# Attention of the sampled rows: forget terms, new keys and new values of four sequences in one product each, key transposes between the score products

## What is computed

```python
def _sample_attention(q, k, v, logf, cache_k, cache_v, cache_logf, page_table):
    ...
    k_all = jnp.concatenate([kp, k], axis=1)
    v_all = jnp.concatenate([vp, v], axis=1)
    f_cum = jnp.cumsum(jnp.concatenate([lp, logf], axis=1), axis=1)
    ...
    out = _attend(q, k_all, v_all, f_cum[:, past:], f_cum, q_pos, k_pos)

def _attend(q, k, v, fq, fk, q_pos, k_pos):
    s = jnp.einsum('nqhd,nkhd->nhqk', q, k).astype(jnp.float32) * (HEAD_DIM ** -0.5)
    s = s + jnp.swapaxes(fq, 1, 2)[..., :, None] - jnp.swapaxes(fk, 1, 2)[..., None, :]
    mask = k_pos[None, :] <= q_pos[:, None]
    s = jnp.where(mask, s, -jnp.inf)
    p = jax.nn.softmax(s, axis=-1)
    return jnp.einsum('nhqk,nkhd->nqhd', p.astype(v.dtype), v)
```

## Time and profile before

| what | value |
|---|---|
| median of three runs | 4012.2 us (4010.51 to 4014.12) |
| profiled execution: its own time | 4016.07 us |
| its span | 4014.3 us |
| mean granted TensorE clock | 0.892 |
| PE busy | 3120.4 us (78%) |
| DVE busy | 2461.1 us (61%) |
| ACT busy | 1553.2 us (39%) |
| POOL busy | 1241.3 us (31%) |
| HBM | 1271.34 MB read, 321 GB/s over the span |

### The profile page before, as it was taken

One profiled execution on the slowest core, in us unless ns is written; L12 is line 12 of the kernel. 1 busy time (PEld: TensorE's weight loads), 2 busy tenths in 40 slices (PEclk: granted clock), 3 DMA queues, 4 the chain that ended last, 5 costly groups with the idle time before them and its releaser, 6 DMA issues. The chain is left out here.

```text
span 4014.3 us, 44298 instructions
## 1 busy us (share of the span) xinstructions
PE 3120.4 (78%) x11756; PEld 1457.5 (36%) x11756; DVE 2461.1 (61%) x6411; ACT 1553.2 (39%) x4273; POOL 1241.3 (31%) x1139
## 2 busy tenths in 40 slices
PE   8799979567886887688678868886887688757777
PEld 2466653243243234224332433242335234411331
DVE  0222221458768758766876677677757775856685
ACT  0233320125534543444255335534552454333333
POOL 0000011013333343443344334433443334334333
PEclk9688889678988999899889989997998899889879
DMA  8211122359998999999999999999999899989998
GB/s 319 77 37 37 37 87 111 120 199 353 408 346 329 409 409 386 370 412 387 386 375 411 390 372 368 405 404 355 400 411 365 351 404 406 376 332 418 371 375 363
DMA packets 299715, 1291.67 MB, mean 322 GB/s; under 512 B 39271, under 2 KB 135415, under 8 KB 163125
## 3 DMA queue, kind: packets, MB, share of 16 engines
q0 software_dynamic: 156672, 1124.27, 69.6%
q1 hardware_dynamic: 142780, 164.51, 12.5%
HBM read 1271.34 MB, written 17.79 MB: 321 GB/s over the span
## 5 line engine op out<-in xcount | busy, mean ns | idle before, releaser
L1647 PE MATMUL YY<-ring,dg 128*64 128x512 f32 (+1 forms) x4224 | 1742.0, 663 | 574.4 <-ACT dg L1218 552.2
L1089 POOL DMA_INDIRECT ring<-experts_dram,idxc x1056 | 1192.0, 1129 | 1925.7 <-PE YY L1647 1721.0
L1492 DVE CUSTOM_DVE_ANT_0 ring<-ring,h2c 128x1024 f32<-128x1024 f32 x1056 | 1266.0, 1225 | 543.0 <-DMA ring<-experts_dram,idxc 533.9
L1647 PEld LDWEIGHTS YY<-ring,dg 128*64 128x64 f32 (+1 forms) x4224 | 519.0, 148 | 1643.9 <-ACT dg L1218 922.6
L1208 ACT ACTIVATE ga<-act 128x1 f32<-128x1 f32 x1056 | 212.1, 201 | 1007.8 <-DVE act L1492 1006.0
L1218 ACT ACTIVATE dg<-fold,gw 128x64 f32<-128x64 f32 x1024 | 356.0, 348 | 50.0 <-PE YY L1647 1.1
L1628 PE MATMUL M<-fT,wq 128*128 128x128 f32 (+1 forms) x2304 | 303.5, 295 | 87.2 <-DMA wq<-w_query_dram 87.2
L1628 PEld LDWEIGHTS M<-fT,wq 128*128 128x128 f32 x2304 | 295.2, 211 | 92.1 <-DMA wq<-w_query_dram 90.8
L1210 ACT ACTIVATE gw<-ga,gc 128x1 f32<-128x1 f32 x1056 | 311.1, 295 | 35.3 <-ACT ga L1208 1.2
L1243 DVE SCALAR_TENSOR_TENSOR yac<-win,cw,yac 128x128 f32<-128x128 f32 x960 | 262.8, 347 | 0.0
L530 PE MATMUL A<-w_in,hT 128*128 128x512 f32 (+1 forms) x432 | 213.8, 660 | 0.0
(11 more groups left out here) (305 smaller groups left out, 2612.6 us busy)
## 6 DMA issues: line engine op xcount, KB each, us to landing
wq<-w_query_dram SPq DMA_DIRECT2D x72, 1024.0 KB, 19.7
wa<-w_ada_dram SPq DMA_DIRECT2D x12, 2048.0 KB, 8.0
ring<-experts_dram,idxc POOLq DMA_INDIRECT x1056, 13.1
w_in<-w_in_dram SPq DMA_DIRECT2D x1, 10272.0 KB, 33.2
kh<-kT_scratch SPq DMA_DIRECT2D x16, 264.0 KB
xb<-x_prompt_dram SPq DMA_DIRECT2D x8, 512.0 KB, 5.3
t_xb<-x_prompt_dram SPq DMA_DIRECT2D x8, 512.0 KB, 11.1
w_o<-w_o_dram SPq DMA_DIRECT2D x8, 512.0 KB, 4.9
```

Source lines behind the costliest of these rows:

```text
L1089: pool.indirect_dma_start(ring[:, k % RING, :], None, I["experts"], bass.IndirectOffsetOnAxis(idxc[:, k:k + 1], 0)).then_inc(g_in[k % RING ...
L1492: v.tensor_tensor_reduce(out=u, in0=u, in1=h2, scale=1.0, scalar=0.0, op0=ALU.mult, op1=ALU.add, accum_out=act8[:, k % RING:k % RING + 1]) ...
L1647: mm = pe.matmul(YY[o, half * 512:(half + 1) * 512], dg[:, k % DG, 0:w], ring[:, k % RING, D + half * 512:D + (half + 1) * 512], start=(k ...
```

## The change

Per group of four sequences instead of per sequence: the forget products (now L811 and L813), the products with the new keys (L816, L817) and those with the new values (L832), each with 128 stationary columns. `Lb` is laid out so that the four sequences of a group lie side by side for each page. `score(n)` becomes `turn(n, c)`, four transposes of one chunk, `meet(n, c)`, one score product, and `forget(g)`. PE's loop transposes chunk c of sequence n and then multiplies chunk c of sequence n − 1. `s_done` is raised after the last score product of a sequence and after `forget(g)`, ten times in all, and the numbers waited for follow that. The products with the values of one sequence now follow those of the sequence before directly.

```diff
-        Lb = sb("Lb", [P, NS * NP, H, QS])
+        Lb = sb("Lb", [P, 2, NP, 4, H, QS])
...
                     if n >= 2:
-                        act.wait_ge(s_done, n - 1)
+                        act.wait_ge(s_done, n - 1 + (n - 2) // 4)
...
-                    own.step(v.tensor_copy(Lb[:, NP * n + j, :, :],
+                    own.step(v.tensor_copy(Lb[:, n // 4, j, n % 4, :, :],
...
                     if n >= 2:
-                        v.wait_ge(s_done, n - 1)
+                        v.wait_ge(s_done, n - 1 + (n - 2) // 4)
...
             def soft(g):
-                v.wait_ge(s_done, 4 * g + 4)
+                v.wait_ge(s_done, 5 * g + 5)
...
-            def score(n):
+            def turn(n, c):
+
+                if c >= 2 or n >= 1:
+                    last = 2 * n + c // 2
+                    pe.wait_ge(kt_dve if c % 2 == 0 else kt_act, last)
+                for j in range(NP):
+                    mm = pe.transpose(T[c % 2][:, j * P:(j + 1) * P], pages[:, NP * n + j, c * P:(c + 1) * P], ident[:, :])
+                mm.then_inc(kt_done, 1)
+
+            def meet(n, c):
                 g, o = n // 4, slice(32 * (n % 4), 32 * (n % 4) + 32)
-                hq = lambda a, m: a[:, m, :, :].rearrange("p h q -> p (h q)")
-                pe.wait_ge(page_in[n], 16 * NP)
+                pe.wait_ge(kt_dve if c % 2 == 0 else kt_act, 2 * n + c // 2 + 1)
+                mm = pe.matmul(SG[g][o, :], Qbd[:, c, n, :, :].rearrange("p h q -> p (h q)"), KT[:, n % 2, c, :],
+                               start=(c == 0), stop=False, skip_group_check=True)
+                if c == CC - 1:
+                    mm.then_inc(s_done, 1)
+
+            def forget(g):
+
+                four = lambda a: a[:, 4 * g:4 * g + 4, :, :].rearrange("p n h q -> p (n h q)")
+                for j in range(NP):
+                    pe.matmul(SG[g][:, :], Lb[:, g, j, :, :, :].rearrange("p n h q -> p (n h q)"),
+                              later[:, 384 - P * j:896 - P * j], start=False, stop=False, skip_group_check=True)
+                pe.matmul(SG[g][:, :], four(L), ones5[:, :], start=False, stop=True, skip_group_check=True)
+                so = OWN[g][:, 0:TS]
                 for c in range(CC):
...
+                    pe.matmul(so, four(Qbd[:, c]), kT[:, c, :], start=(c == 0), stop=False)
+                pe.matmul(so, four(L), later32[:, :], start=False, stop=True).then_inc(s_done, 1)
...
                     for j in range(NP):
-                        pe.matmul(OG[o, :], PT[:, g, j, o], pages[:, NP * n + j, DA:2 * DA], start=(j == 0), stop=False)
-                    mm = pe.matmul(OG[o, :], PTo[:, g, o], vs[:, :], start=False, stop=True)
-                mm.then_inc(o_done, 1)
+                        pe.matmul(OG[o, :], PT[:, g, j, o], pages[:, NP * n + j, DA:2 * DA], start=(j == 0), stop=False,
+                                  skip_group_check=True)
+                pe.matmul(OG[:, :], PTo[:, g, :], vs[:, :], start=False, stop=True, skip_group_check=True).then_inc(o_done, 1)
...
-            for n in range(NS):
-                score(n)
+            for n in range(NS + 1):
+                if n < NS:
+                    pe.wait_ge(page_in[n], 16 * NP)
+                for c in range(CC):
+                    if n < NS:
+                        turn(n, c)
+                    if n:
+                        meet(n - 1, c)
+                if n % 4 == 0 and n:
+                    forget(n // 4 - 1)
                 if n == 5:
                     values(0)
             values(1)
```

More of the change, by code:

```diff
@@ L788, in _ @@
             pe.matmul(OG[:, :], hrow[:, :], hcol[:, :], start=True, stop=True).then_inc(masks_done, 1)
-            def score(n):
-                g, o = n // 4, slice(32 * (n % 4), 32 * (n % 4) + 32)
-                hq = lambda a, m: a[:, m, :, :].rearrange("p h q -> p (h q)")
-                pe.wait_ge(page_in[n], 16 * NP)
-                for c in range(CC):
[L796 to L812, removed]
```

## The result

The changed kernel takes 3961.6 us (median of four runs, 3957.3 to 3964.3) against 4011.4 (four runs, 4010.0 to 4014.1): a ratio of 0.9873, 95% interval 0.9852 to 0.9893. It gained 49.7 us where 43.6 were forecast. The direction and the place were right; the size was 6 us short, and the median lies at the very edge of the range that began at 3961. By the ratio of the runs, 0.9873 of the 4012.2 that was given, it is 3961.2. That this is just inside is luck: the edge stood for free changes of shape, short passes at their old pace and the runs' spread, and neither of the first two came.

What follows compares the result with a forecast made beforehand. TensorE was taken to set the pace of the `sampled` stage. Terms 29.1 + 12.1 − 2.0 + 9.4 − 5.0 = 43.6 us gained, giving a median of 3968.6 us; range 3961 to 3976, carried to 3982 for two rivals.

Steps and rivals of the forecast that it cites:

- Where it lies and what bounds it: The closed stage `sampled`, 148 of 4014 us: TensorE sets its pace, and what it gains the whole program gains.
- Forget term and new keys: Once per four sequences: eight blocks of 5.04 us go, two of 5.6 come; gain 29.1 us.
- Transposes between products: Score products interleaved with the next sequence's transposes: gain 12.1 us, less 2.0 for new holes and 5.0 for shape changes.
- So the holes of sequences 1 to 7 go: PE's waits for KT copies vanish through interleaving: six of 1.67 us and 2.13 for sequence 6, gain 12.1.
- New values: In values(g), products with new values once per four sequences: 4.7 us per group, gain 9.4, crossings between column quarters included.
- Three crossings: 1.3: In values(g), each crossing between column quarters lays one pass over another, 0.44 us each, read from the last stage.
- nothing: Other end for the crossings in values(g): no overlap of column quarters, 2.6 us less gain.
- The new hole of sequence 5: Before its third lot of transposes, PE waits because soft(0) stands ahead of keys(5) on DVE: 1.4 us lost.
- the wait at the start: Sequence 1's transposes must wait for its pages, 599.7 where sequence 0's products started at 599.13: 0.6 us lost.
- Dear changes of shape: Rival, 6%: each of the 56 changes between transposes and score products costs 0.31 us, 12.4 more, 3981.0 us.
- No hiding: Rival, 6%: key copies come too late for interleaving to hide transposes; 12.1 us not gained, 2.0 not spent, 3978.7 us.
- The clock: Rival, 4%: transposes between products keep TensorE at 1.2 GHz; 64.6 us lost if throughout, 4033.2 us.

Runs made afterwards that it cites:

- bare_turns: Changed kernel with all sixteen transposes of a sequence before its four score products again, the rest as changed; stage 94.56 us against 96.70.
- one_quarter: Changed kernel with all page products of values(g) written to the first 32 partitions of OG, one column quarter; stage 108.66 us against 96.70.
- pairs: Changed kernel reworked: sequences two at a time through two banks, values(g) with page loop outside, softmaxes moved; stage 74.13 us against 96.70, median 3946.2 us.
- values_old: Changed kernel with the products with the new values per sequence again, as before the change; stage 112.40 us against 96.70.

## Why the prediction was right or wrong

**Where it lies and what bounds it: right.** TensorE paced the stage, and 49.15 of the 49.7 us are in it. By undoing the parts, the new values gave 6.3 us more than forecast, the forget term and the turns 0.4 and 0.9 less.

**Forget term and new keys: right.** 29.1 forecast, 28.7 by undoing it. The block is 6.03 us, not 5.6: the rows give 3.63 for the four products with `later`, 1.05 for that with `ones5`, 1.01 for eight short passes (0.126 each, where I had 0.11) and 0.34 for the last two with the change back.

**Transposes between products: a sum that came near by luck, with the wrong reason.** 12.1 − 2.0 − 5.0 = 5.1 forecast, and undoing both halves gives 6.3 − 2.1 = 4.2. The step that failed is "So the holes of sequences 1 to 7 go", where it puts all of them down to the interleaving. They did go, but of the 1.67 us of a sequence, 0.85 were the wait for all four copies ahead of a product that needs the first; the moved wait takes them away in either order, 6.3 us in the stage. The interleaving itself hides the other hole, and pays for it with 28 pairs of changes at 0.275 us, 7.7 us instead of 5.0, with the hole behind `soft(0)`, and with the start: the first score product comes 5.64 us after the first transposes (590.06 to 595.70), since the pages of sequence 1 must land before it, where in bare_turns it comes after 3.82 (588.04 to 591.86). It loses 2.1 us. Nor did I see that a rival lay there: this half of the change was worth doing without. For the change from transposes to products I had 0.06 us from the four transposes followed by one of 32 columns; that was from one transpose to another. From a transpose to a product it is 0.585 − 0.43 = 0.155. Why these two differ, no run tells apart.

**New values: the term that was mis-sized.** 9.4 forecast, 15.7 measured by undoing it (17.4 read straight from before to after, see the end). The step is "Three crossings: 1.3. I take it, since it is the same pattern". It was the same pattern and another bound. ACT's timeline in the stretch of the earlier trace rows:

```profile
1522.07 0.35 ACT L1218 ACTIVATE dg<-fold,gw 128x64 f32<-128x64 f32 x1
...
1523.20 0.35 ACT L1218 ACTIVATE dg<-fold,gw 128x64 f32<-128x64 f32 x1
...
1524.35 0.35 ACT L1218 ACTIVATE dg<-fold,gw 128x64 f32<-128x64 f32 x1
```

and a weight load of the products there:

```profile
1522.46 0.19 PEld L1647 LDWEIGHTS YY<-ring,dg 128*64 128x64 f32 x2 [0.57 <-ACT dg L1218]
```

ACT makes a `dg` each 1.15 us, and the first load of each four passes waits for one: the `dg` of 1522.07 is done at 1522.42, the load starts at 1522.46, and the next two blocks of four start at 1523.60 and 1524.74, each 0.05 us after the end of their `dg` as well. The products could not follow closer whatever the array allowed, so 1.15 instead of 1.72 us per four passes was the rate of the feeder. Freed of it, 32 passes take 8.79 us instead of 12.4, and in the right order 3.58. (Those are quarters; what halves would do with a faster feeder, no run shows.) The other end of this term, "nothing", was no help either: the range was open only towards less gain, and it was more.

**The new hole of sequence 5** was 1.1 us, 1.4 forecast; the wait at the start, 595.11 against a landing at 595.09, as forecast.

**The rivals.** Dear changes of shape: 0.14 us each on average, not 0.31. No hiding: no holes with KT copies in sequences 1 to 4. The clock (its price was read a little high: the eight passes from 715.42, in the row below, took 6.26 us against 3.55, not twice as long): from 594.5 to 599.9 the changed kernel's granted clock was 1.00, and score passes kept coming 0.43 us apart, so the half level that transposes were to bring did not come; it went down only where it did before, around the softmax of group 1 (0.57 from 668 to 672). But the lower clock does reach this order of work: in one_quarter, with the same transposes and products, it was 0.66 from 594 to 599, behind 2.05 us of idling for pages, and in pairs 0.50 from 602.2 to 608.9, with 2.94 us of such idling in it. So the rival's price is real where the pages come late, though not for the reason it gave.

The undone parts add up: 28.7 + 15.7 + 6.3 − 2.1 = 48.6 of 49.15 us. They agree better than they are known, since the lower clock lasts differently in group 1's values. The same eight passes, in the kernel before and in values_old:

```profile
715.42 6.34 PE L825 MATMUL OG<-pages,PT 128*32 128x512 f32 x8 [1.09 <-DVEq L753]
...
683.77 5.03 PE L830 MATMUL OG<-pages,PT 128*32 128x512 f32 x8 [1.09 <-DVEq L753]
```

With the same order of work, from the first transposes of `values(1)` to the sending took 26.85 us before and 25.15 in values_old. Read straight from before to after, the values part is 8.25 us in group 0 and 9.12 in group 1 (26.85 to 17.73), 17.4 and not 15.7. In the same way the forget terms and new keys come to 28.3 (8 × 5.04 − 2 × 6.03), and 3.5 of the 49.15 are left for the turns. By either reading the new values are the term that was far too small.

## What to carry to other kernels

Products that fill only a quarter of the array's columns took here, four at a time, the time of one, when they went to four different quarters in turn with nothing of another shape between: put the loop over the quarters innermost. Before interleaving two kinds of work to hide a wait, ask first whether the wait is for more than the next instruction needs, and count the changes of shape that the interleaving adds. And a rate read from a stretch says what the array can do only if nothing feeds that stretch more slowly; look at who makes its operands before using it as a price or as an end of a range.

## What was not expected of the hardware

- Passes of f32 products with 128 rows and 32 columns run four at a time into the four column quarters: 32 passes of 512 columns in 3.58 us, against 13.85 into one quarter.
- Blocks of eight passes per quarter, one after another, still overlap by about four passes at each crossing (8.79 us), and lose it all to one product with 32 rows between them (4.52 us per block of eight and that product).
- A pair of changes between transposes and products with 32 columns costs 0.275 us: 0.155 into the product, 0.12 back.
